# Two edits in a two-block transformer kernel: how the first weight unit and the second tile of x are loaded and split, and where the second gate tile stands

## What is computed

```python
h = rmsnorm(x, attn_norm[l])
z = h @ w_in[l]                     # pool input 1024, q 1024, k 128, v 128, gates 2048
gates = sigmoid(z[..., o4:] + b_gate[l])
a = pool_mixer(u_pool, w_pool[l], pool_scale[l])   # four groups: windowed mean minus input, then a 256 x 256 product
b = swa_sink_attention(q, k, v, sinks[l])          # 16 heads, window 128
x = x + (g_pool * a + g_attn * b) @ w_out[l]
```

## Time and profile before

| | us |
|---|---|
| median of three runs (1426.73 to 1429.03) | 1426.79 |
| the profiled execution, device time | 1428.66 |
| its span, from the first to the last instruction | 1426.9 |
| PE busy | 1367.3 (96%), 7492 matmuls |
| POOL busy | 897.8 (63%) |
| DVE busy | 712.5 (50%) |
| ACT busy | 440.8 (31%) |

### The profile page before, as it was taken

How to read it: one execution, slowest core, us unless ns; L and a number is a source line. 1 busy time by engine, 2 the same in 40 slices (tenths; PEclk the granted TensorE clock), 3 DMA queues, 4 the chain that set the end, 5 groups by cost and what they waited for, 6 DMA issues and landing times.

```text
span 1426.9 us, 20886 instructions
## 1 busy us (share of the span) xinstructions
PE 1367.3 (96%) x7492; PEld 1115.5 (78%) x7492; DVE 712.5 (50%) x1151; ACT 440.8 (31%) x886; POOL 897.8 (63%) x1042
## 2 busy tenths in 40 slices
PE   7999999899999999999899999899999999999996
PEld 5877777688888887888778886649788888888884
DVE  7878766734444445112668875595655111211113
ACT  3343444423221212111345455624533111111111
POOL 6856644387777777777375854414267776777772
PEclk9999999999999999999999999999999999999998
DMA  5321321133232232233121111000032323232321
GB/s 194 109 84 59 92 69 63 45 101 109 89 102 90 101 97 95 90 101 98 35 89 60 46 60 51 24 1 2 17 102 74 116 90 103 89 103 89 102 88 59
DMA packets 31888, 113.78 MB, mean 80 GB/s; under 512 B 3536, under 2 KB 3920, under 8 KB 31696
## 3 DMA queue, kind: packets, MB, share of 16 engines
q1 hardware_dynamic: 31680, 112.72, 24.1%
q10 hardware_dynamic: 144, 0.18, 0.0%
HBM read 110.79 MB, written 2.10 MB: 79 GB/s over the span
## 4 chain that ended last, share of the span: by engine, by line
PE 85%; DVE 7%; ACT 3%; issue 3%; POOL 1%; DMA 0%; SPq 0%; DVEq 0%; POOLq 0%; ACTq 0%
PE ps L1099 42%; PE ps L1351 19%; PE ps L1489 6%; ACT arena L581 3%; PE ps L1118 1%; PE ps L1371 1%; PE ps L1463 1%; PE ps L1153 1%; PE ps L1184 1%; PE ps L1289 1%; PE ps L1251 1%; PE ps L1443 1%; PE ps L1162 1%; PE ps L1741 1%; PE ps L1694 1%
## 5 line engine op out<-in xcount | busy, mean ns | idle before, releaser
L494 POOL TENSOR_TENSOR w_lo<-raw,w_hi 128x256 fp32r<-128x256 f32 (+1 forms) x804 | 646.8, 834 | 42.5 <-ACT w_hi L581 26.5
L486 POOL TENSOR_SCALAR w_hi<-raw 128x1024 fp32r<-128x1024 f32 (+1 forms) x188 | 201.6, 1073 | 393.0 <-issue 338.6
L1099 PE MATMUL ps<-h_hi,w_hi 128*128 128x512 f32 x912 | 362.6, 398 | 1.2 <-POOL w_lo L494 1.1
L1099 PE MATMUL ps<-h_hi,w_lo 128*128 128x512 f32 x912 | 355.3, 390 | 0.0
L1099 PE MATMUL ps<-h_lo,w_hi 128*128 128x512 f32 x912 | 355.2, 389 | 0.0
L1099 PEld LDWEIGHTS ps<-h_hi,w_hi 128*128 128x128 f32 x912 | 171.2, 188 | 46.1 <-issue 7.4
L1099 PEld LDWEIGHTS ps<-h_lo,w_hi 128*128 128x128 f32 x912 | 171.2, 188 | 37.8 <-issue 3.0
L1099 PEld LDWEIGHTS ps<-h_hi,w_lo 128*128 128x128 f32 x912 | 171.2, 188 | 36.0
L581 ACT ACTIVATE arena<-arena 128x512 f32<-128x512 f32 (+6 forms) x194 | 102.5, 531 | 185.0 <-DVE arena L2519 119.2
L1351 PE MATMUL ps<-g_hi,w_hi 128*128 128x512 f32 x400 | 155.7, 389 | 0.9 <-DVE arena L2119 0.9
L1351 PE MATMUL ps<-g_hi,w_lo 128*128 128x512 f32 x400 | 155.6, 389 | 0.0
(11 more groups left out here) (299 smaller groups left out, 1934.2 us busy)
## 6 DMA issues: line engine op xcount, KB each, us to landing
raw<-in_w_stream SPq DMA_DIRECT2D x204, 512.0 KB, 3.5
out<-xT SPq DMA_DIRECT2D x8, 256.0 KB, 2.1
xT<-in_x_t SPq DMA_DIRECT2D x1, 1056.0 KB, 8.2
xT<-in_x_t SPq DMA_DIRECT2D x1, 792.0 KB, 6.1
arena<-in_cst SPq DMA_DIRECT2D x1, 528.0 KB, 4.3
C<-in_cst SPq DMA_DIRECT2D x1, 448.0 KB, 9.4
xT<-in_x_t SPq DMA_DIRECT2D x1, 264.0 KB, 3.8
arena<-in_pos SPq DMA_DIRECT2D x1, 256.0 KB, 3.8
```

Of the source, the lines that this page charges most:

```text
L486: pool.tensor_scalar(w_hi[j][:, k0:KT, :], raw[j % 2][:, k0:KT, :], 1.0, 1.0, ALU.mult, ALU.mult).then_inc(S["pool_step"], 1)
L494: low = pool.tensor_tensor(w_lo[j][:, k:k + n, :], raw[j % 2][:, k:k + n, :], w_hi[j][:, k:k + n, :], ALU.subtract)
L1099: last = mm(dst[p], w[:, k, :], h[:, k, cols], start=(k == 0 and n == 0), stop=(k == KT - 1 and n == 2))
```

## The change

Three things are done. Unit 0 is loaded in two halves, with tile 1 of x between them, and ACT and POOL wait for each piece by itself; tiles 2 and 3 of x follow in one transfer. POOL subtracts the low part of unit 0 in four instructions and no longer in one. The second gate tile (unit 21) is multiplied in two parts, k = 0..2 ahead of `pooled(0)` and k = 3..7 behind it. Two later transfers share a semaphore, of which both readers now wait for the full count.

```diff
-                    sp.dma_start(raw[j % 2][:].rearrange("p a b -> p (a b)"),
-                                 w_stream[ds(4 * i + j), :, :].rearrange("a p n -> p (a n)")
-                                 ).then_inc(raw_ready[j % 2], 16)
+                    if isinstance(i, int) and i == 0 and j == 0:
+                        sp.dma_start(raw_j[:, 0:512], unit_j[:, 0:512]).then_inc(S["raw_first"], 16)
+                        sp.dma_start(xT[:, 1:2, :], x_t[:, 1:2, :]).then_inc(S["x_second"], 16)
+                        sp.dma_start(raw_j[:, 512:1024], unit_j[:, 512:1024]).then_inc(raw_ready[0], 16)
+                    else:
+                        sp.dma_start(raw_j, unit_j).then_inc(raw_ready[j % 2], 16)
...
-                            sp.dma_start(xT[:, 1:4, :], x_t[:, 1:4, :]).then_inc(S["x_loaded0"], 16)
+                            sp.dma_start(xT[:, 2:4, :], x_t[:, 2:4, :]).then_inc(S["x_loaded0"], 16)
                             sp.dma_start(xT[:, 4:8, :], x_t[:, 4:8, :]).then_inc(S["x_loaded1"], 16)
...
-            sp.dma_start(arena[:, p4 + 2 * L + 640:p4 + 4 * L + 640], cst2).then_inc(S["c2_loaded"], 16)
-            sp.dma_start(wba32, w_ba).then_inc(S["ba_loaded"], 16)
+            sp.dma_start(arena[:, p4 + 2 * L + 640:p4 + 4 * L + 640], cst2).then_inc(S["misc_loaded"], 16)
+            sp.dma_start(wba32, w_ba).then_inc(S["misc_loaded"], 16)
...
-                    pool.wait_ge(raw_ready[j % 2], 16 * (2 * i + j // 2 + 1))
+                    if isinstance(i, int) and i == 0 and j == 0:
+                        pool.wait_ge(S["raw_first"], 16)
+                    else:
+                        pool.wait_ge(raw_ready[j % 2], 16 * (2 * i + j // 2 + 1))
...
                             pool.tensor_scalar(w_hi[0][:, 0:4, :], raw[0][:, 0:4, :], 1.0, 1.0, ALU.mult, ALU.mult).then_inc(S["w_first"], 1)
+                            pool.wait_ge(raw_ready[0], 16)
...
-                    n = KT if isinstance(i, int) and i == 0 else 2
+                    n = KT if isinstance(i, int) and i == 0 and j > 0 else 2
...
             a(h_hi5[:, 0, :], xT[:, 0, REAL], ACT.Copy, scale=vcol("attn_norm", 0)).then_inc(S["hi_ready"], 1)
+            act.wait_ge(S["x_second"], 16)
+            a(h_hi5[:, 1, :], xT[:, 1, REAL], ACT.Copy, scale=vcol("attn_norm", 1)).then_inc(S["hi_ready"], 1)
             for p in range(2):
                 act.wait_ge(S[f"x_loaded{p}"], 16)
-                for f in range(4 * p + 1 - p, 4 * p + 4):
+                for f in range(4 * p + 2 - 2 * p, 4 * p + 4):
...
+            def gate_part(i, ks):
+
+                u = U_GATE + i
+                if ks.start == 0:
+                    pe.wait_ge(S["tile_read"], 18 + i - 1)
+                    pe.wait_ge(split_done[u % 4], rounds(u))
+                for k in ks:
+                    for n, (w, h) in enumerate(((w_hi, h_hi5), (w_hi, h_lo5), (w_lo, h_hi5))):
+                        last = mm(ps[:, i % 2, :], w[u % 4][:, k, :], h[:, k, :], start=(k == 0 and n == 0), stop=(k == KT - 1 and n == 2))
+                if ks.stop == KT:
+                    last.then_inc(unit_done[u % 4], 1)
...
             pe.wait_ge(S["v_ready"], 1)
+            gate_part(1, range(0, 3))
             pooled(0)
-            gate(1)
+            gate_part(1, range(3, 8))
             pe.wait_ge(S["qk_dve"], 9)
...
-            dve.wait_ge(S["ba_loaded"], 16)
+            dve.wait_ge(S["misc_loaded"], 64)
...
-            dve.wait_ge(S["c2_loaded"], 16)
+            dve.wait_ge(S["misc_loaded"], 64)
```

More of the change, by code:

```diff
@@ L302, in build @@
         names = (
-            "x_first w_first x_loaded0 x_loaded1 v_loaded c_loaded misc_loaded c2_loaded ba_loaded out_done "
+            "x_first x_second raw_first w_first x_loaded0 x_loaded1 v_loaded c_loaded misc_loaded out_done "
             "pool_step act_step dve_step "
@@ L432, in load @@
                         sp.wait_ge(split_done[j + 2], i)
-                    sp.dma_start(raw[j % 2][:].rearrange("p a b -> p (a b)"),
-                                 w_stream[ds(4 * i + j), :, :].rearrange("a p n -> p (a n)")
-                                 ).then_inc(raw_ready[j % 2], 16)
+                    raw_j = raw[j % 2][:].rearrange("p a b -> p (a b)")
+                    unit_j = w_stream[ds(4 * i + j), :, :].rearrange("a p n -> p (a n)")
+                    if isinstance(i, int) and i == 0 and j == 0:
[4 more added lines that the diff above has]
+                        sp.dma_start(raw_j, unit_j).then_inc(raw_ready[j % 2], 16)
                     if isinstance(i, int) and i == 0:
                         if j == 0:
-                            sp.dma_start(xT[:, 1:4, :], x_t[:, 1:4, :]).then_inc(S["x_loaded0"], 16)
+                            sp.dma_start(xT[:, 2:4, :], x_t[:, 2:4, :]).then_inc(S["x_loaded0"], 16)
                             sp.dma_start(xT[:, 4:8, :], x_t[:, 4:8, :]).then_inc(S["x_loaded1"], 16)
```

## The result

The change made the kernel slower. Median of 20 runs 1429.36 us (1425.98 to 1431.56), beside 1426.26 us (1425.02 to 1429.11) for the kernel before, run beside it; ratio of the runs 1.0014, 95% interval 1.0008 to 1.0020, that is +2.0 us (+1.1 to +2.9). The two medians themselves are 3.1 us apart, the two means (1428.88 and 1426.52) 2.4. A second set of 12 runs of the same kernel gave 1428.56 beside 1427.08, ratio 1.0010 (1.0001 to 1.0019), means 1.4 us apart. I had forecast 1426.0 and a range up to 1428.2. Two later executions of the kernel before, 1959.55 and 5111.65 us, were in a slow state and are left out of all that follows.

What follows compares the result with a forecast made beforehand. PE, busy 96% of the span, was taken as the bound, with a chain ahead of it setting the start. Start -0.65 and second site -0.16 sum to -0.81: 1426.79 - 0.81 = 1426.0 us, range 1423.7 to 1428.2.

Steps and rivals of the forecast that it cites:

- (a): Start, x loads: tiles 2 and 3 land when tiles 1 to 3 did, about 7.8 us; cost 0, bound 0.3 us.
- my own sign: Profile after, start: tiles 2 and 3 of x landing later than 8.1 us would show the forecast wrong.
- rival 3: Start gives nothing because tiles 2 and 3 land 0.65 us or more late: 1426.6 us, possibly slower; chance 0.07.
- ACT's 0.65: Start: tile 1's copy leaves ACT's run behind the landing, so everything after it comes 0.65 us earlier.
- (b): Start: tiles 4 to 7 of x, landed at 10.35, are there when ACT needs them at 11.14; cover 0.8 us.
- (d): Start: POOL's unit 0 work gets 0.95 us longer, 3.3 for 2.35, covered by its idle time from 9.88 to 15.34.
- (c): Start: DVE is free at about 11.8 us for tile 4's `h_lo5`; 0.1 us of cost is the bound.
- PE's 0.56 of slack stays: Start, before unit 2: PE's work comes 0.65 us earlier too, so its 0.56 us wait for POOL remains.
- The second site, -0.16: Pooled groups: stall moves from 1.93 us before `pooled(0)` to about 1.85 before `pooled(1)`, gaining 0.16 us of work.
- The clock there, term 0: Pooled groups: the half-clock stretch moves along with the stall to `pooled(1)`, so 0; bounds -1.7 and +1.7 us.
- Rival 2: At or behind `pooled(1)`: the moved stall brings a half-clock stretch the old one mostly didn't, +1.7 us: 1427.7; chance 0.2.
- rival 4: Elsewhere, as at 966.6 or 1055.4: shifting PE also removes half-clock stretches, 1.7 or 3.4 us each: 1422 to 1423.9; chance 0.08.

Runs made afterwards that it cites:

- products of ones: Useless ones-matrix products added on PE while it waits at the start: in the kernel before 1428.93 us (ratio 1.0014), in the whole change 1429.57 us (1.0017).
- start as before, k = 0..2 or 0, 1 (four): Kernel before with only the gate tile split, two sets each: k = 0..2 ahead of `pooled(0)` 1427.92 and 1428.03 us; k = 0, 1 ahead 1426.63 and 1426.77.
- four parts and the wait: Kernel before with unit 0's low part in four instructions and PE starting tile 1 only when tile 2's low part is made: 1426.34 us, ratio 0.9999.
- tile 1 of x by itself: Kernel before with only tile 1 of x in its own transfer, behind the whole of unit 0: 1427.11 us, ratio 1.0000.
- the same with k = 0, 1: Kernel before with tile 1 of x in its own transfer behind whole unit 0, and gate tile k = 0, 1 ahead of `pooled(0)`: 1427.13 us, ratio 0.9998.
- the change and the wait: Whole change, with PE starting tile 1 only when tile 2's low part is made too: 1428.69 us, ratio 1.0010 against the kernel before.
- unit 0 by partitions: Kernel before with only unit 0 loaded in two transfers, partitions 0 to 63 and 64 to 127, POOL waiting for both: one run, 1429.62 us.
- four parts alone: Kernel before with only the low part of unit 0 in four instructions, loads and gate tile as before: 1427.95 us, ratio 1.0009.
- the start alone: The change with the gate tile whole again: unit 0 in two loads around tile 1 of x, four low parts: 1428.85 us, ratio 1.0012 against before.
- unit 0 in halves, twice: Kernel before with only unit 0 loaded in two column halves, then tiles 1 to 3 of x in one transfer: single runs, 1430.45 and 1431.10 us.

## Why the prediction was wrong, point by point

**(a) Tiles 2 and 3 land in time: failed, the largest step.** I took 0 with 0.3 as the bound; the landing was 1.08 late, and 0.7 to 1.4 in the four other executions with this start. By my own sign (a landing later than 8.1) the step was wrong, and rival 3, to which I gave 0.07, describes what happened here. I had read the full queue, landings 2.6 us apart for 1056 KB, as proof that a cut costs nothing. Those rows show two large transfers in a row, not a small one cut in two. The fixed part of about 2.0 us for each transfer that I took from the Trainium skill, DMA: Bandwidth & Descriptors (it stands in the section Anatomy of one DMA, as a fit to transfers issued by GpSimd; here SP issues them), was right in its direction: the cut of unit 0 cost 1.0 to 1.3 us, that of x 0.4. With it two cuts would cost up to 4; measured, 0.7 to 1.4. The measurement decides, and it lies between my row and the Trainium skill.

**ACT's 0.65:** right in size (1.33 for 1.95), used up by the landing. POOL's unit 1 started at 15.81, 0.47 later, where I had said 0.65 earlier.

**(b) and (d):** the covers held. POOL's four parts of unit 0 took 3.48 us (estimate 3.3), covered by its idle time. **(c)** DVE was in time. But the step asked the wrong question: whether DVE is done with tile 3, and not at what pace PE gets tiles 1 to 3.

**"PE's 0.56 of slack stays": failed.** I never priced PE's clock at the start. The profiles of all starts without products of ones, against before (POOL's unit 1 at 15.34, `qk_side(8)` at 126.04); the third column has the start of the last product that is followed at 0.43 us or more:

| execution | POOL's unit 1 later by | last product at the lower spacing | `qk_side(8)` later by |
|---|---|---|---|
| before | 0 | 13.34 | 0 |
| start as before, k = 0..2 or 0, 1 (four) | -0.11 to -0.05 | 15.07 to 15.96 | -0.12 to 0.02 |
| four parts and the wait | -0.07 | 15.11 | 0.01 |
| tile 1 of x by itself | -0.22 | 15.82 | -0.32 |
| the same with k = 0, 1 | -0.10 | 14.22 | -0.23 |
| the change and the wait | 0.37 | 15.55 | 0.38 |
| the change again | 0.13 | 15.74 | 0.23 |
| unit 0 by partitions | 0.99 | 14.33 | 1.03 |
| four parts alone | 0.01 | 16.89 | 0.26 |
| the start alone | 0.20 | 17.09 | 0.47 |
| the change | 0.47 | 17.78 | 0.87 |
| unit 0 in halves, twice | 1.04, 1.27 | 18.35, 19.01 | 1.53, 1.83 |

Where the last such product starts before 16 us, PE is late by what POOL is late, within about 0.1. Where it starts later, PE becomes the bound and 0.25 to 0.56 us are added. The slack itself I had read from one execution: with the start as before PE's wait of 0.56 us before unit 2 is gone in the four other profiles, as the clock rises later in them, and PE is no later for it.

Does work in drips delay the rise? In all five executions where it starts after 16 us PE was idle again between its tiles 1 and 4. But in three more with such gaps it starts at 14.22, 15.74 and 15.82, among those without. So it is a tendency in these profiles; the mean of the added wait fits it, with the reserve made there. That all 1.5 us of the start's cost are this and the landing isn't shown: the four executions with this start and no products of ones are 0.2 to 0.9 late at `qk_side(8)`.

**The second site, -0.16:** right in mechanism, and the gain measured is twice as large. From `qk_side(8)` to the first transposes takes 21.45 us after and 21.79 in a kernel with the old order and no half clock at this place (126.05 to 147.84): -0.34. The stall was moved as the working said, 1.80 for an expected 1.85.

**The clock there, term 0: failed.** I let the old stretch move along to `pooled(1)`. It never came there. Of the nine profiles with the old order seven have it at 130 us. Of the six with k = 0..2 none has it there or at `pooled(1)`, but two have one at 149, two at 272, and two a second one at 691, places where none of the nine has one (of the three with k = 0, 1 one has it at 272). Over the runs k = 0..2 has 0.7 of a stretch more than before. The term was about +1 and not 0. Rival 2 had this sign and a price, 1427.7, though not the place. Gate tile and start measured alone give 0.8 + 1.5 = 2.3, the start being the larger part, which I had put at -0.65; the whole change measured 2.0 (1.1 to 2.9), by the means 2.4 in the first set and 1.4 in the second. The errors of these sums are near 1 us, so that they fit is no proof that nothing else is in it. Why a stall of 1.8 us before `pooled(1)` costs more clock than one of 1.93 before `pooled(0)` stays open. What is shown is only that two short stalls, 0.40 and 1.14, cost nothing that 22 runs can tell.

**A sum of rival 4** was off: one or two such stretches less give 1424.3 or 1422.6, not 1422 to 1423.9. Nothing rested on it.

## What to carry to other kernels

A transfer that stands at the head of a full queue is not free to cut: look at when the transfer behind it lands, and try the cut alone. Work that reaches PE earlier but in drips can be worse than the same work later in one piece (1428.10 and 1426.73 in the means here); read the spacing of the products, since the column of the granted clock did not show it at the start. And a stall that is filled from behind itself opens where the filling came from: prefer two short ones to one long one, and judge by many runs: the first profile after was of an execution 2.9 us below the median of its kernel.

## What the runs showed of the hardware that I had not expected

- Unit 0 in two transfers, by columns or by partitions, delayed the next landing by 1.0 to 1.3 us, with the engines counted busy. Between 4 and 8 us the rate was 292 to 406 GB/s with the halves of columns and fell to 193 to 298 for three of these four microseconds with the cut by partitions, against 428 to 444 before.
- DVE and POOL with one long instruction (2.35 us) serve DVE's three in 1.91 and twice 0.7; with four short ones they take turns, 1.0 to 1.2 us for each of DVE's, with the same sum, 3.25 us. Cutting POOL's instruction changes who is first, not DVE's total; POOL's own grows from 2.35 to 3.69 us.
- At the start of the span the granted clock reads 1.00 while the products stand 0.43 us apart.
